# Attention and the output projection of one decoder layer on one core: the product with v a step later, row turnings inside the products

## The chip, the cores and the metric

The kernel runs on one core of one Trainium2 chip. The metric is the device time of one execution in microseconds; the times shown are medians of several runs. Lower is better.

## The reference, cut to what matters

One layer of a decoder for 2048 prompt tokens and 8 x 4 decode tokens, all in float32. Attention is "stick breaking": no softmax, but a product over the keys behind.

```python
z = einsum('bqhd,bkhd->bhqk', q, k) * HEAD_DIM_SB ** -0.5 + sb_bias
mask = k_pos[None, :] < q_pos[:, None]
log_1mb = where(mask, log_sigmoid(-z), 0.0)
suffix = cumsum(log_1mb, axis=3, reverse=True) - log_1mb
a = where(mask, exp(log_sigmoid(z) + suffix), 0.0)
o = einsum('bhqk,bkhd->bqhd', a, v)
...
hp = hp + mix_merge(o_sb, o_mlp, gn_sb, gn_mlp, w_out)      # two RMS norms, one projection
y, conv_p = conv_ffn(rmsnorm(hp), ...); hp = hp + y          # 1024 -> 2 x 2816 -> 1024
hp = per_layer_embedding(hp, p, ...)
y_prompt = rmsnorm(hp, final_norm_g)
```

There are 8 heads of 64; the decode tokens attend to 2048 cached keys, held in pages of 128 that a page table names.

## The kernel before, in words

Four stages follow each other: `project_mlp`, `project_qk`, `attend`, `finish_tokens`. Products in full precision are made of float32 operands split into a high and a low part (`k_hi`, `k_lo`, `w_hi`, `w_lo`): ScalarE casts the high part, VectorE subtracts it for the low part, and TensorE makes two or three products.

**attend.** One step is one block of 128 queries of one head against its i + 1 tiles of 128 keys (i = 0 to 15); there are 128 steps, written out by hand, and every engine walks through them in order. Step t does several things for different blocks. TensorE makes the logits of block t into `ps_z` (`logits`, L959 to L963), turns the weights of block t - 3 in groups of four tiles into the three banks `ps_t` (`turn`, L969), and makes their product with v into `ps_o` (`weigh`, L981). ScalarE makes two sigmoids out of each bank pair of logits (L1104, L1106), copies each turned group from `ps_t` to `aT` (`take`, L1093) and each finished quad of blocks to `oT` (`quad_out`, L1116). VectorE runs the scan over the keys of block t - 1 (`product`, L1211) and the weights of block t - 2 (`weights`, L1216). One turned group goes ahead of the logits (up to three, where no keys are turned), the others behind them; the product with v follows at once.

The decode tokens are worked in the same steps, in two groups of four sequences of 54 units each, spread over the steps by a count of keys (`units_of`, at most a few units a step): 32 units of key pages (TensorE turns two pages a unit, L991, ScalarE copies one and VectorE the other, L1284; every fourth unit also makes logits, L1001), one for the new keys, one scan, one for the weights, two for turning, 16 sums with v pages (L1034; VectorE adds each to `own`, L1268) and one mix. All turned blocks, keys, logits and sums share the three banks in one fixed order (`fill_at`). GpSimd issues the page loads (L930) into a ring of 9 pages, each when the page 9 before it has been used. SP loads the q and k of a whole head (`load`, L870: four pieces of 512 KB) into one raw buffer once the previous head's are split; ScalarE casts k at i = 5 (`keys_high`, L1111), VectorE splits q at i = 5 to 7 and k at i = 8 (L1185 to L1206).

**finish_tokens.** Five blocks of 416 tokens. Per block: the output projection in 8 products of 8 k-tiles x 3 matmuls (L58 to L60, `product`), the feed-forward pair, and the embedding gate. Weights arrive in slabs of 512 KB; ScalarE casts them (`high`, L1568), VectorE subtracts (`low`, L1729), four slots each. The finished rows of block b - 1 leave during the output projection of block b: VectorE normalises 8 tiles (L1796), then, between the fourth and fifth product, `turn_out` turns them in 8 groups of four into two banks (L1487), and ScalarE's `way_out` copies each group (L1630) and issues its store (L1635). VectorE then adds the residual (L1751), which frees the accumulator that the fifth product needs.

Of the kernel before, what the change touches and what calls it, by code (L numbers as in the profile page):

```python
# [700 lines left out]
def attend(nc, keep, T, D):  # L701
# [4 lines left out]
    GROUPS, PB, PAGES, RING = 2, 4, 16, 9  # L706
# [5 lines left out]
    HIGH_PARTS, LOW_PART = 5, 8  # L712
    FIRST = BANK

    def has(s):
        return 0 <= s < STEPS
# [21 lines left out]
    units_of = [[] for _ in range(STEPS + LAG + 1)]  # L738
    t, run, placed = 3, keys_of(3) + 300, 0
    for g in range(GROUPS):  # L740
        for u in range(UNITS):
            if apart(u) and units_of[t]:
                t += 1
                run += keys_of(t) + 300
# [36 lines left out]
    for t in range(STEPS + LAG):  # L781
# [7 lines left out]
    with ExitStack() as ctx:  # L789
        m = Alloc(nc, ctx, "at")  # L790
        k_raw, q_raw = m.sb("k_raw", [P, 2048]), m.sb("q_raw", [P, 2048])
# [4 lines left out]
        aT = [m.sb(f"aT{s}", [P, 4, P]) for s in range(4)]  # L796
# [8 lines left out]
        v_new = m.sb("v_new", [4 * PB, GROUPS, BANK])  # L805
# [12 lines left out]
        loaded, k_high, head_high, head_low, z_ready, b_done, product_done, a_done = (  # L818
            m.sem(n) for n in ("loaded", "k_high", "head_high", "head_low", "z_ready", "b_done", "product_done", "a_done"))
        o_ready, o_out, made, cast, rest_zeroed = (m.sem(n) for n in ("o_ready", "o_out", "made", "cast", "rest_zeroed"))  # L820
        first_loaded, first_k_high, first_q_high, first_ready = (
            m.sem(n) for n in ("first_loaded", "first_k_high", "first_q_high", "first_ready"))
# [7 lines left out]
        v_src = T["v_prompt"][0, 0].rearrange("(kt p) h d -> p kt h d", p=P)  # L830
        caches = [T[n][0].rearrange("n p h d -> p n (h d)") for n in ("cache_k", "cache_v")]
# [31 lines left out]
        with nc.Block() as block:  # L863

            @block.sync
            def _(sp):
                def load(h):
                    for raw, src in ((k_raw, D["KT"]), (q_raw, D["QT"])):
                        for half in range(2):
                            sp.dma_start(raw[64 * half:64 * half + 64, :], src[64 * h:64 * h + 64, :]).then_inc(loaded, 16)  # L870

                def load_first(raw, src, c0, c1, signal):
                    for half in range(2):
                        sp.dma_start(raw[64 * half:64 * half + 64, c0:c1], src[0:64, c0:c1]).then_inc(signal, 16)
# [9 lines left out]

                load_first(k_raw, D["KT"], 0, FIRST, first_loaded)
                load_first(k_raw, D["KT"], FIRST, 2048, loaded)
# [1103 lines left out]
```

## Time and profile before

| | |
|---|---|
| median of 3 runs | 3399.02 us (3394.91 to 3401.98) |
| the profiled execution, its own time | 3402.7 us |
| its span | 3401.1 us |
| mean granted TensorE clock | 0.975 |
| TensorE busy | 3206.0 us |
| VectorE busy | 2106.0 us |
| ScalarE busy | 1645.8 us |

The span runs from the first to the last instruction. Busy time is the union of an engine's instructions; matmuls are pipelined, so that a record lasts longer than the distance to the next one, and a busy TensorE isn't one at its peak. PE is TensorE, DVE VectorE, ACT ScalarE, POOL GpSimd; L981 is line 981 of the kernel.

### The profile page before, as it was taken

What the parts mean: (1) busy time and instruction counts of PE and PEld (TensorE: products, weight loads), DVE (VectorE), ACT (ScalarE), POOL (GpSimd) and SP (SyncE); (2) the same over time, 40 slices, a digit from 0 to 9 for tenths busy, and PEclk for the clock granted to TensorE, in tenths of its full rate; (3) what the DMA queues carried; (4) which work ended last, traced back from release to release, by engine and by line L of the source; (5) the groups of instructions that cost most, each with busy time, mean ns of one, the idle gap of its engine ahead of it and who ended that gap; (6) DMA issues with size and microseconds to landing.
All of it is one profiled execution on the core that took longest, in us unless ns stands there. A gap on an engine that the chain in (4) does not pass through costs nothing.

```text
span 3401.1 us, 51867 instructions
## 1 busy us (share of the span) xinstructions
PE 3206.0 (94%) x18462; PEld 2941.2 (86%) x18462; DVE 2106.0 (62%) x2865; ACT 1645.8 (48%) x2305; POOL 146.5 (4%) x275
## 2 busy tenths in 40 slices
PE   8999897788989989799999999999999999999997
PEld 6888686677777767699998999899998999989996
DVE  4222322678877787577476764777656775678845
ACT  5434211676667666445344443454444543445433
POOL 0000000111221111000000000000000000000000
PEclk9999898899999999899999999999999999999998
DMA  5222334642654333543444333543335433433331
GB/s 174 91 93 71 117 108 116 160 106 71 168 145 111 98 106 97 169 123 115 116 136 141 117 113 113 154 126 118 110 104 171 122 117 113 141 115 116 115 116 59
DMA packets 575191, 405.62 MB, mean 119 GB/s; under 512 B 37498, under 2 KB 538659, under 8 KB 573187
## 3 DMA queue, kind: packets, MB, share of 16 engines
q1 hardware_dynamic: 532660, 298.24, 30.7%
q0 software_dynamic: 20480, 67.13, 6.8%
q10 hardware_dynamic: 21872, 37.92, 3.3%
q8 instruction: 108, 1.77, 0.2%
q14 instruction: 71, 0.57, 0.1%
HBM read 358.34 MB, written 44.87 MB: 119 GB/s over the span
## 4 chain that ended last, share of the span: by engine, by line
PE 57%; DVE 1%; ACT 1%; issue 0%; ACTq 0%; DMA 0%; DVEq 0%
PE pf_acc L60 19%; PE pf_acc L58 19%; PE pf_acc L59 18%; PE pf_ps_sum L1449 0%; ACTq L1635 0%; ACT pf_c L1630 0%; DMA pf_mix<-MIXT 0%; ACT pf_u L1630 0%; PE pf_ps_t L1487 0%; DVE pf_h L1914 0%; DVE pf_u L1735 0%; ACT pf_sq L1575 0%; DVE pf_h L1751 0%; DVE pf_h L1796 0%; DVE pf_ssum L1745 0%
## 5 line engine op out<-in xcount | busy, mean ns | idle before, releaser
L58 PE MATMUL pf_acc<-pf_x_hi,pf_w_hi 128*128 128x416 f32 x2080 | 732.0, 352 | 2.4 <-DVE pf_h L1751 2.4
L60 PE MATMUL pf_acc<-pf_x_hi,pf_w_lo 128*128 128x416 f32 x2080 | 734.2, 353 | 0.0
L1568 ACT ACTIVATE pf_w_hi<-pf_raw 128x1024 fp32r<-128x1024 f32 x440 | 464.7, 1057 | 541.8 <-PE pf_acc L60 538.7
L59 PE MATMUL pf_acc<-pf_x_lo,pf_w_hi 128*128 128x416 f32 x2080 | 725.9, 349 | 0.0
L1729 DVE TENSOR_TENSOR pf_w_lo<-pf_raw,pf_w_hi 128x1024 fp32r<-128x1024 f32 x440 | 536.8, 1221 | 283.0 <-ACT pf_w_hi L1568 282.8
L58 PE MATMUL pf_acc<-pf_f_hi,pf_w_hi 128*128 128x416 f32 x1280 | 456.4, 357 | 11.1 <-DVE pf_w_lo L1729 8.0
L60 PE MATMUL pf_acc<-pf_f_hi,pf_w_lo 128*128 128x416 f32 x1280 | 455.7, 356 | 0.0
L59 PE MATMUL pf_acc<-pf_f_lo,pf_w_hi 128*128 128x416 f32 x1280 | 451.3, 353 | 0.0
L59 PEld LDWEIGHTS pf_acc<-pf_x_lo,pf_w_hi 128*128 128x128 f32 x2080 | 390.8, 188 | 8.1 <-issue 1.6
L58 PEld LDWEIGHTS pf_acc<-pf_x_hi,pf_w_hi 128*128 128x128 f32 x2080 | 390.4, 188 | 7.1 <-issue 5.0
L60 PEld LDWEIGHTS pf_acc<-pf_x_hi,pf_w_lo 128*128 128x128 f32 x2080 | 390.0, 188 | 2.2
L1211 DVE TENSOR_TENSOR_SCAN at_rest<-at_rest 128x127 f32<-128x127 f32 (+15 forms) x128 | 309.2, 2416 | 26.3 <-ACT at_rest L1106 26.0
L981 PE MATMUL at_ps_o<-at_aT,at_v 128*64 128x128 f32 x2176 | 276.7, 279 | 45.9 <-ACT at_aT L1093 41.6
L981 PEld LDWEIGHTS at_ps_o<-at_aT,at_v 128*64 128x64 f32 x2176 | 237.0, 138 | 71.5 <-ACT at_aT L1093 51.7
L58 PEld LDWEIGHTS pf_acc<-pf_f_hi,pf_w_hi 128*128 128x128 f32 x1280 | 243.7, 190 | 17.2 <-DVE pf_w_lo L1729 9.2
L59 PEld LDWEIGHTS pf_acc<-pf_f_lo,pf_w_hi 128*128 128x128 f32 x1280 | 243.8, 190 | 5.5 <-issue 1.3
L60 PEld LDWEIGHTS pf_acc<-pf_f_hi,pf_w_lo 128*128 128x128 f32 x1280 | 243.3, 190 | 1.8
L1093 ACT ACTIVATE at_aT<-at_ps_t 128x512 f32<-128x512 f32 (+2 forms) x320 | 157.8, 536 | 136.8 <-PE at_ps_t L969 136.5
L969 PE MATMUL at_ps_t<-keep_ident,at_rest 128*128 128x128 f32 x1088 | 159.5, 282 | 28.9 <-DVE at_rest L1216 28.3
L1104 ACT ACTIVATE at_beta<-at_ps_z,at_bias 128x1024 f32<-128x1024 f32 (+2 forms) x192 | 166.6, 868 | 25.9 <-PE at_ps_z L960 16.4
L969 PEld LDWEIGHTS at_ps_t<-keep_ident,at_rest 128*128 128x128 f32 x1088 | 122.2, 144 | 63.8 <-DVE at_rest L1216 47.5
L58 PE MATMUL pa_ps_acc<-pa_w_hi,pa_x_hi 128*128 128x512 f32 x408 | 164.6, 403 | 6.8 <-DVE pa_w_lo L480 6.8
(225 smaller groups left out, 4394.3 us busy)
## 6 DMA issues: line engine op xcount, KB each, us to landing
pf_raw<-in_w_up_dram SPq DMA_DIRECT2D x220, 512.0 KB, 3.8
pf_raw<-in_w_down_dram SPq DMA_DIRECT2D x80, 512.0 KB, 4.0
at_pages<-in_cache_k_dram POOLq DMA_DIRECT2D x128, 256.0 KB, 3.2
at_pages<-in_cache_v_dram POOLq DMA_DIRECT2D x128, 256.0 KB, 3.2
pf_raw<-in_w_out_dram SPq DMA_DIRECT2D x40, 512.0 KB, 5.2
pf_raw<-in_w_ple_gate_dram SPq DMA_DIRECT2D x40, 512.0 KB, 4.0
pf_raw<-in_w_down_dram SPq DMA_DIRECT2D x40, 384.0 KB, 3.4
pf_mix<-MIXT ACTq DMA_DIRECT2D x5, 1664.0 KB, 9.4
```

Source lines behind the costliest of these rows:

```text
L58: nc.tensor.matmul(out, stat_hi, mov_hi, start=first, stop=False)
L59: nc.tensor.matmul(out, stat_hi, mov_lo, start=False, stop=False)
L60: return nc.tensor.matmul(out, stat_lo, mov_hi, start=False, stop=last)
L969: last = nc.tensor.transpose(bank[:, kt % 4 * P:kt % 4 * P + P], rest[s % 4][:, kt * P:(kt + 1) * P], keep["ident"][:, :])
L981: last = nc.tensor.matmul(ps_o[0:64, i % 4 * P:(i % 4 + 1) * P], v[h % 2][:, kt, :], aT[group(s, r) % 4][:, kt % 4, :], start=kt == 0, sto ...
L1093: nc.scalar.activation(out, src, ACT.Copy).then_inc(emptied_by(key), 1)
L1104: nc.scalar.activation(beta[t % 3][:, 1024 * g:1024 * g + w], ps_z[at % 2][:, 0:w], ACT.Sigmoid, bias=bias[t // NQ % 2][:, :])
L1211: nc.vector.tensor_tensor_scan(r, r, r, 1.0, ALU.mult, ALU.min).then_inc(product_done, 1)
L1568: nc.scalar.activation(w_hi[k % 4][:, :], raw[k % 4][:, :], ACT.Copy).then_inc(hi_split, 1)
L1729: nc.vector.tensor_tensor(w_lo[k % 4][:, :], raw[k % 4][:, :], f32(w_hi[k % 4][:, :]), ALU.subtract).then_inc(lo_split, 1)
```

## The change

In `attend`, the product with v of block s is made one step later (`weigh(s - 1)`), and all turned groups of a step stand in one run ahead of the logits. `aT` gets 8 slots instead of 4. ScalarE makes all copies out of the three banks: both pages of a key unit, and each sum, which goes to a buffer `stage` that VectorE then adds from, behind its scan and weights. q and k are loaded, cast and split by halves of 1024 columns into raw buffers of half the size: the first half of the next head at i = 10 to 12, the second half of the current head at i = 4 to 6. The ring has 8 pages instead of 9, and `v_new` is loaded by GpSimd, per group. In `finish_tokens`, the 8 groups of turnings stand inside the third, fourth and fifth product (`TURNS`), the first half of the tiles first, each followed by its own copy and store on ScalarE; VectorE adds the residuals of the first four tiles as soon as that half is turned and makes their low parts one tile behind.

```diff
-    GROUPS, PB, PAGES, RING = 2, 4, 16, 9
+    GROUPS, PB, PAGES, RING = 2, 4, 16, 8
...
-    HIGH_PARTS, LOW_PART = 5, 8
-    FIRST = BANK
+    HALF, FIRST = 1024, BANK
+    PART_AT = (10, 4)
+    SLOTS = 8
...
-        return min(groups[s], max(1, 3 - len(turned_fills(t)))) if has(s) else 0
+        return groups[s] if has(s) else 0
...
-        k_raw, q_raw = m.sb("k_raw", [P, 2048]), m.sb("q_raw", [P, 2048])
+        k_raw, q_raw = m.sb("k_raw", [P, HALF]), m.sb("q_raw", [P, HALF])
...
-        aT = [m.sb(f"aT{s}", [P, 4, P]) for s in range(4)]
+        aT = [m.sb(f"aT{s}", [P, 4, P]) for s in range(SLOTS)]
...
-                def load(h):
+                def load(n):
+                    h, c0 = n // 2, n % 2 * HALF
+                    sp.wait_ge(half_ready, n)
...
+                    if h + 1 < HEADS:
+                        load(2 * h + 2)
                     store(h, 0)
                     store(h, 1)
-                    if h + 2 < HEADS:
-                        sp.wait_ge(head_low, h + 2)
-                        sp.wait_ge(head_high, 3 * h + 6)
-                        load(h + 2)
+                    if h + 1 < HEADS:
+                        load(2 * h + 3)
...
+                                if part == 1 and k + bi == 0:
+                                    if g:
+                                        wait_filled(pool, ("sum", g - 1, PAGES - 1))
+                                    pool.dma_start(v_new[:, :], new_rows[16 * g:16 * g + 16, :]).then_inc(new_loaded, 16)
...
+                    if i == (4 if h == 0 else 0) and g == 0:
+                        pe.wait_ge(half_ready, 2 * h + 1)
+                    if i == 8 and g == 0:
+                        pe.wait_ge(half_ready, 2 * h + 2)
...
-                        weigh(s)
+                    if has(s - 1):
+                        weigh(s - 1)
...
+                def keys_high(n):
+                    h, c0 = n // 2, n % 2 * HALF
+                    act.wait_ge(loaded, 64 * n + 64)
+                    nc.scalar.activation(k_hi[h % 2][:, c0:c0 + HALF], k_raw[:, :], ACT.Copy).then_inc(k_high, 1)
...
+                    if U_SUM <= u < U_MIX:
+                        key, n = ("sum", g, u - U_SUM), PAGES * g + u - U_SUM
+                        if n >= 2:
+                            act.wait_ge(summed, n - 1)
+                        wait_filled(act, key)
+                        nc.scalar.activation(stage[n % 2][:, :], bank_of(key)[:, :], ACT.Copy).then_inc(emptied_by(key), 1)
...
+                        for bi in (2 * (u % 2), 2 * (u % 2) + 1):
+                            k, key = u // 2, ("key", g, u // 2, bi)
+                            copy_out(key, kT[:, bi, :, k % 2 * P:k % 2 * P + P], bank_of(key)[:, :].rearrange("p (h t) -> p h t", h=4))
...
-                    if quad_end(s - 1):
-                        quad_out((s - 1) // 4)
+                    if quad_end(s - 2):
+                        quad_out((s - 2) // 4)
...
+                    if t % NQ == PART_AT[0] and t // NQ + 1 < HEADS:
+                        keys_high(2 * (t // NQ + 1))
+                    if t % NQ == PART_AT[1] and t < STEPS:
+                        keys_high(2 * (t // NQ) + 1)
...
+                def operands(n, part, first=0):
+                    slot = n // 2 % 2
+                    src = slice(first, HALF)
+                    cols = slice(n % 2 * HALF + first, n % 2 * HALF + HALF)
                     if part == 0:
-                        dve.wait_ge(loaded, 64 * h + 64)
-                        done = nc.vector.tensor_copy(q2[slot][:, c0:], q_raw[:, c0:])
-                    elif part == 1:
-                        dve.wait_ge(head_high, 3 * h + (1 if h else 2))
-                        done = nc.vector.tensor_tensor(q2[slot][64:P, c0:], q_raw[64:P, c0:], f32(q2[slot][64:P, c0:]), ALU.subtract)
-                    else:
-                        nc.vector.tensor_scalar(bias[slot][:, :], keep["sb_bias"][:, h:h + 1], 1.0, None, ALU.mult)
-                        done = nc.vector.tensor_scalar(minus_bias[slot][:, :], keep["sb_bias"][:, h:h + 1], -1.0, None, ALU.mult)
-                    done.then_inc(head_high, 1)
+                        dve.wait_ge(loaded, 64 * n + 64)
+                        nc.vector.tensor_copy(q2[slot][:, cols], q_raw[:, src]).then_inc(q_high, 1)
+                    if part == 1:
+                        dve.wait_ge(q_high, n + 1)
+                        nc.vector.tensor_tensor(q2[slot][64:P, cols], q_raw[64:P, src], f32(q2[slot][64:P, cols]), ALU.subtract)
+                        if n % 2 == 0 and n:
+                            biases_of(n // 2)
+                    if part == 2:
+                        dve.wait_ge(k_high, n + 1)
+                        nc.vector.tensor_tensor(k_lo[slot][:, cols], k_raw[:, src], f32(k_hi[slot][:, cols]), ALU.subtract).then_inc(half_ready, 1)
...
-                        k, bi = u // 2, 2 * (u % 2) + 1
-                        key = ("key", g, k, bi)
-                        wait_filled(dve, key)
-                        nc.vector.tensor_copy(kT[:, bi, :, k % 2 * P:k % 2 * P + P], bank_of(key)[:, :].rearrange("p (h t) -> p h t", h=4))\
-                            .then_inc(emptied_by(key), 1)
...
+                    for g, u in units_of[t - 1] if t else ():
+                        sample_sums(g, u)
+                    if t == 1:
+                        for part in range(3):
+                            operands(0, part, FIRST)
+                    for half in range(2):
+                        part, h = t % NQ - PART_AT[half], t // NQ + 1 - half
+                        if 0 <= part < 3 and h < HEADS:
+                            operands(2 * h + half, part)
...
+    TURNS = {2: {5: 0, 7: 1}, 3: {1: 2, 3: 3, 5: 4, 7: 5}, 4: {1: 6, 3: 7}}
...
+                        if i == 7:
+                            last.then_inc(slab_done, 1)
+                        if i in groups:
+                            turn_out(b, groups[i])
...
-                        if mt == 4 and behind:
-                            turn_out(b - 1)
...
+                def turn_out(b, n):
+
+                    half, tt = divmod(n, 4)
+                    w = P if tt < 3 else 32
+                    pe.wait_ge(y_ready, 8 * b + 4 * half + 4)
+                    pe.wait_ge(y_copied, 8 * b + n + 1)
+                    for k in range(4):
+                        done = nc.tensor.transpose(ps_t[n % 2][0:w, k * P:(k + 1) * P], h[:, 4 * half + k, tt * P:tt * P + w], keep["ident"][:, :])
+                    done.then_inc(y_turned, 1)
...
+                        for cast, groups in ((4, ()), (5, (0, 1)), (6, (2, 3))):
+                            high(q4, O_AT + cast)
+                            for n in groups:
+                                way_out(b - 1, behind_at, False, n)
                     for mt in range(8):
                         residual(b, 0, mt, OU, G_FFN, (q4, O_AT + mt + 4) if mt >= 4 or behind_at is None else None)
+                        if behind_at is not None and mt < 4:
+                            if mt == 1:
+                                high(q4, O_AT + 7)
+                            way_out(b - 1, behind_at, False, 4 + mt)
...
+                    if norm == 0 and mt % 4 == 0 and not isinstance(b, int):
+                        dve.wait_ge(y_turned, 8 * b + mt - 3)
...
+                    for mt in range(4 if behind else 0):
                         done(q4, O_AT + mt)
-                        residual(b, 0, mt, OU, G_FFN, (q4, O_AT + mt + 4) if mt >= 4 or not behind else None)
+                        add_residual(b, 0, mt, OU)
+                        if mt:
+                            low_residual(b, 0, mt - 1, G_FFN)
+                    if behind:
+                        low_residual(b, 0, 3, G_FFN)
+                        low(q4, O_AT + 7)
```

## Rows read from the trace of the kernel before

**Rows 1.** Busy us, share of the span and instructions, from the page.

```profile
PE 3206.0 (94%) x18462; PEld 2941.2 (86%) x18462; DVE 2106.0 (62%) x2865; ACT 1645.8 (48%) x2305; POOL 146.5 (4%) x275
```

**Rows 2.** Windows of two stages: length, busy us per engine, clock, DMA share, GB/s.

```profile
588.00:1368.00 780.00, 689.37 (x5442) 558.96 (x5442) 582.45 (x414) 524.85 (x836) 138.02 (x256) 0.96 0.44 118
1368.00:3401.00 2033.00, 1971.02 (x10324) 1926.93 (x10324) 1343.53 (x2093) 930.31 (x1152) 0.13 (x1) 0.98 0.42 123
```

**Rows 3.** TensorE's waits from 588 to 1368: us in total, times, longest.

```profile
PE at_ps_o L981 <- ACT at_aT L1093: 41.6, 36, 10.6
PE at_ps_t L969 <- DVE at_rest L1216: 28.3, 16, 6.6
...
PE at_ps_t L1034 <- DMA at_pages<-in_cache_v_dram: 6.4, 4, 5.0
PE at_ps_t L991 <- DMA at_pages<-in_cache_k_dram: 5.1, 1, 5.1
```

**Rows 4.** Timeline of TensorE, one step: start, us, instructions [idle before].

```profile
727.46 0.43 PE L981 MATMUL at_ps_o<-at_aT,at_v 128*64 128x128 f32 x2 [1.13 <-ACT at_aT L1093]
727.82 1.09 PE L991 MATMUL at_ps_t<-keep_ident,at_pages 128*128 128x128 f32 x8
...
730.75 1.09 PE L981 MATMUL at_ps_o<-at_aT,at_v 128*64 128x128 f32 x8
732.77 0.65 PE L981 MATMUL at_ps_o<-at_aT,at_v 128*64 128x128 f32 x4 [0.93 <-ACT at_aT L1093]
733.35 1.09 PE L991 MATMUL at_ps_t<-keep_ident,at_pages 128*128 128x128 f32 x8
```

**Rows 5.** Timeline of ScalarE in the same step.

```profile
729.39 0.60 ACT L1093 ACTIVATE at_aT<-at_ps_t 128x512 f32<-128x512 f32 x1 [0.28 <-PE at_ps_t L969]
...
731.34 1.11 ACT L1106 ACTIVATE at_rest<-at_ps_z,at_minus_bias 128x1023 f32<-128x1023 f32 x1
732.33 0.38 ACT L1093 ACTIVATE at_aT<-at_ps_t 128x256 f32<-128x256 f32 x1
```

**Rows 6.** Last stage, turning of rows: three windows (as rows 2), then two copies of ScalarE.

```profile
1797.24:1807.77 10.53, 6.34 (x35) 3.78 (x34) 1.82 (x2) 5.11 (x8) 0.00 (x0) 0.77 0.76 241
1807.77:1813.13 5.36, 5.36 (x15) 5.11 (x16) 2.26 (x5) 2.75 (x5) 0.00 (x0) 0.50 0.25 89
1813.13:1818.49 5.36, 5.36 (x30) 5.29 (x29) 3.94 (x9) 3.16 (x6) 0.00 (x0) 0.99 0.00 0
...
1798.15 0.60 ACT L1630 ACTIVATE pf_c<-pf_ps_t 128x512 f32<-128x512 f32 x1 [3.99 <-PE pf_ps_t L1487]
...
1799.39 0.60 ACT L1630 ACTIVATE pf_c<-pf_ps_t 128x512 f32<-128x512 f32 x1 [0.64 <-ACT pf_c L1630]
```

**Rows 7.** Timeline of TensorE at the end of the kernel.

```profile
3384.14 6.79 PE L1487 MATMUL pf_ps_t<-keep_ident,pf_h 128*128 128x128 f32 x28 [1.13 <-DVE pf_h L1796]
```

**Rows 8.** Head 0: TensorE's timeline, then a window (as rows 2).

```profile
620.28 1.97 PE L981 MATMUL at_ps_o<-at_aT,at_v 128*64 128x128 f32 x8 [10.63 <-ACT at_aT L1093]
...
620.30:626.00 5.70, 5.70 (x25) 4.95 (x25) 5.33 (x5) 3.28 (x5) 0.87 (x2) 0.56 0.05 15
```

**Rows 9.** VectorE in attention, by line: busy us, mean ns, idle before.

```profile
L1211 DVE TENSOR_TENSOR_SCAN at_rest<-at_rest 128x127 f32<-128x127 f32 (+15 forms) x128 | 309.2, 2416 | 26.3 <-ACT at_rest L1106 26.0
...
L1284 DVE COPY at_kT<-at_ps_t 128x512 f32<-128x512 f32 x64 | 44.2, 691 | 108.2 <-PE at_ps_t L991 108.1
```

**Rows 10.** Head 1: its window (as rows 2), and TensorE's waits in it.

```profile
695.50:792.50 97.00, 90.14 (x744) 74.73 (x744) 71.84 (x52) 68.88 (x110) 15.02 (x28) 0.98 0.41 109
...
PE at_ps_o L981 <- ACT at_aT L1093: 6.1, 7, 1.4
PE at_ps_t L969 <- DVE at_rest L1216: 2.1, 1, 2.1
```

**Rows 11.** Landings: all loads of L870 (512 KB each), and one kind of DMA.

```profile
DMA to landing us min/median/max: 5.2/9.6/15.1
...
at_k_raw<-KT SPq DMA_DIRECT2D x2, 128.0 KB, 3.8
```

More of the change, by code:

```diff
@@ L737, in attend @@
     total_keys = sum(keys_of(s) + 300 for s in range(3, STEPS - 2))
-    units_of = [[] for _ in range(STEPS + LAG + 1)]
+    units_of = [[] for _ in range(STEPS + LAG + 2)]
     t, run, placed = 3, keys_of(3) + 300, 0
@@ L742, in attend @@
             if apart(u) and units_of[t]:
-                t += 1
-                run += keys_of(t) + 300
+                for _ in range(2 if u == U_MIX else 1):
+                    t += 1
+                    run += keys_of(t) + 300
             while t < STEPS - 3 and run * GROUPS * UNITS < placed * total_keys:
@@ L804, in attend @@
         q_block, k_new = m.sb("q_block", [P, 4, PB, 32]), m.sb("k_new", [P, 4, 4 * PB])
-        v_new = m.sb("v_new", [4 * PB, GROUPS, BANK])
+        v_new = m.sb("v_new", [4 * PB, BANK])
+        stage = [m.sb(f"stage{n}", [P, BANK]) for n in range(2)]
         beta_s, rest_s = m.sb("beta_s", [P, KEYS + 4]), m.sb("rest_s", [P, KEYS + 4])
@@ L1069, in _ @@
                 pe.wait_ge(cast, 2)
-                for t in range(STEPS + LAG):
+                for t in range(STEPS + LAG + 1):
                     s = t - LAG
@@ L1146, in _ @@
                 act.sem_inc(oT_stored[1], 16)
-                for c0, c1, signal in ((0, FIRST, first_loaded), (FIRST, 2048, loaded)):
-                    for half in range(2):
-                        act.dma_start(q_raw[64 * half:64 * half + 64, c0:c1], D["QT"][0:64, c0:c1]).then_inc(signal, 16)
+                for c0, c1, signal in ((0, FIRST, first_loaded), (FIRST, HALF, loaded)):
+                    for part in range(2):
+                        act.dma_start(q_raw[64 * part:64 * part + 64, c0:c1], D["QT"][0:64, c0:c1]).then_inc(signal, 16)
                 nc.scalar.activation(warm[:, :], keep["eps"][:, :], ACT.Sigmoid)
@@ L1153, in _ @@
                 act.wait_ge(rest_zeroed, 4)
-                for t in range(STEPS + LAG + 1):
+                for t in range(STEPS + LAG + 2):
                     s = t - LAG
@@ L1299, in _ @@
                 first_operands()
-                for t in range(STEPS + LAG + 1):
-                    for g, u in units_of[t - 1] if t else ():
-                        sample_sums(g, u)
+                for t in range(STEPS + LAG + 2):
                     for g, u in units_of[t]:
@@ L1455, in mix_mean_square, with product @@
                     nc.tensor.matmul(ps_sum[:, 0:TB], keep["mean512"][:, :], c[0][:, 0:TB], start=True, stop=True).then_inc(mix_sum, 1)
-                def product(q4, k, unit, mov_hi, mov_lo, order=range(8), ready=None):
+                def product(q4, k, unit, mov_hi, mov_lo, order=range(8), ready=None, groups={}, b=None):
                     for i, kt in enumerate(order):
@@ L1549, in _ @@
                 mean_square(21 * NB)
-                turn_out(NB - 1)
+                for n in range(8):
+                    turn_out(NB - 1, n)
                 for n in range(6):
@@ L1713, in _ @@
                 root(NB - 1, 2)
-                way_out(NB - 1, (NB - 1) * TB, True)
+                for n in range(8):
+                    way_out(NB - 1, (NB - 1) * TB, True, n)
                 for n in range(6):
@@ L1758, in residual @@
                     add_square(b, norm, mt)
+                def residual(b, norm, mt, unit, gain, between=None):
+                    add_residual(b, norm, mt, unit)
+                    if between and mt < 7:
+                        low(*between)
+                    low_residual(b, norm, mt, gain)
                     if between and mt == 7:
```

151 lines of the change are left out of this document (50 added, 101 removed).

## The prediction

> **What bounds the kernel now.** I read the page's busy table first. TensorE is busy 94% of the span [rows 1], so what counts is where TensorE stands still. The windows by stage put that in one place: between 588 and 1368 us (attention) TensorE is busy 689.4 of 780 us, VectorE 582.5, ScalarE 524.9; in the last stage it is busy 1971 of 2033 us [rows 2]. The diff touches those two stages and no other.
>
> The waits of TensorE inside attention [rows 3] say what ends its pauses. 41.6 us in 36 pauses end with ScalarE's copy of a turned block: the product with v of a step follows its own turnings at once. 28.3 us in 16 end with VectorE's weights; 6.4 and 5.1 us end with pages that land late.
>
> The timeline of one middle step [rows 4] shows the mechanism. TensorE turns keys at 727.82, starts the product with v at 730.75, runs out after eight matmuls and goes on only at 732.77; the next step starts at 733.35. The eight show 1.09 us busy and two show 0.43; the six more cost 0.66, 0.11 each. The ninth could have begun at 730.75 + 8 x 0.11 = 731.63; the real loss is 1.14 against 0.93 shown. I add 0.2 to each such pause. ScalarE [rows 5] is then inside two sigmoids of 1024 (1.11 each, 1.0 apart) and reaches the last block's copy at 732.33.
>
> In the last stage I looked for the same thing at the turning of the finished rows, once per block of tokens [rows 6]. From 1797.24 to 1807.77 there is no product at all: eight groups of four turnings alternate with ScalarE's copies, whose starts are 1.24 apart. Then 15 matmuls take 5.36 us at a granted clock of 0.50 (1.2 GHz); the next 30 take the same time at 0.99 (2.4 GHz).
>
> **The last stage, costed.** After the change the eight groups stand inside the third, fourth and fifth product, two k-tiles apart. Removed per block: 10.53 us, and the slow start after it, 15 matmuls of 0.36 instead of 0.18, 2.7 us. Added: 32 turnings between products. Four turnings are issued in about 0.5 us (eight key turnings of the same size show 1.09 in rows 4 like eight products with v, so 0.12 each), so 8 x 0.5 = 4.0. The gate of the groups is ScalarE: copy 0.6 and DMA issue 0.4 make 1.24 per group; groups are 6 x 0.18 + 0.5 = 1.6 apart on TensorE, so ScalarE keeps up while it has nothing else. It also has two casts and the residual's two passes over a tile, each about as long as a copy or two, between the groups from the third on. Following its order, only the eighth group's bank is late, by some 0.4; I take 0.7. Sum per block: 10.53 + 2.7 - 4.0 - 0.7 = 8.5, four times 34. VectorE's new order (residual 0 only after group 4 of the first half) frees the fifth product's bank about 2 us before it is wanted. At the end of the kernel the groups go half by half, so that the first four need only four normalised tiles: the second group waited 1.13 more for the other half [rows 7], 1.2 gained. **35 us**, bounds 26 (each group at ScalarE's pace once more: 2 us a block) and 38.
>
> For the slow start: the Trainium skill (TensorE: Matmul & The Clock Gate, Terms) gives the penalty of a throttled time as that time times (1 - K/N), here one half. Applied to the throttled time of a block, which reaches back into the turnings (0.77 in the 10.53 us before, rows 6), it would give more than the 2.7 us that the row shows. By the row, only the throttled part in which products run dense counts, and I go by the row.
>
> **Attention, what is removed.** (a) 35 of the 36 pauses behind ScalarE's copies, 31.0 us, plus 0.2 each, 7: 38. Product s-1 uses copies made a step ago, and eight slots of aT keep them.
> (b) The 36th, 10.63 us at 620.28, is something else: ScalarE had to cast head 1's k and, in order behind that, copy this step's block; the load of 2 MB landed late [rows 8]. Now 1 MB is wanted at that point, it is released sooner (operands of the first half are ready at step 1, not 3, and SP no longer issues v_new in front of it), and 1 MB of head 0 is no longer ahead of it. I leave 2.5 us of it: 8 gained, bounds 4 and 10.6. After it TensorE ran 5.7 us at a clock of 0.56, 2.5 us lost, gained too. The page wait of 5.1 just before: 2 gained.
> (c) VectorE's 28.3 us. Its scans, 309 us, and the weights stay [rows 9]. It no longer copies half the keys (44 us) and no longer stands behind TensorE's key turnings (108 us idle, rows 9), so it starts on a step's scan earlier. The longest, 6.6 us, stands behind the scan of the decode part; there are two such, 13 us, and they stay. Of the other 15 us I take half, 8; bounds 3 and 15.
> (d) Pages of v, 6.4 us, in 4 pauses, the longest 5.0, while a 2 MB head load was under way: 3 gained; a ring of 8 pages instead of 9 gives at most 2 us back at the step with two sums.
> Removed: 38 + 8 + 2.5 + 2 + 8 + 3 = 61.5.
>
> **Attention, what is added.** ScalarE gets 64 key copies and 32 copies of sums. In a run they start 0.5 apart (0.60 shown; an instruction of 1.11 in rows 5 is followed after 0.99, so some 0.1 overlaps), 48 us over the stage; 525 + 48 = 573 of about 735. In head 1 [rows 10] TensorE needs 97.0 less its stops of 6.1 + 2.1 and 8 x 0.2: 87.2; ScalarE 68.9 + 14 x 0.5 = 76; VectorE 71.8 - 14 x 0.6 = 63.5. TensorE stays the bound over the head, but not in each step. With 9 to 13 key tiles ScalarE has 1.0 (keys) + 1.0 to 1.3 (blocks) + 2.0 + 0.5 to 1.4 (sigmoids), and 0.95 more where half of k is cast (1024 columns, like a sigmoid of rows 5): 4.2, 4.6, 5.8, 5.3, 5.6. TensorE has 4.1 (733.35 - 727.82 = 5.53 in rows 4, less the stop of 1.14 and one tile less to weigh), 4.5, 4.9, 5.4, 5.9. All turnings come before the logits and share three banks, so a late ScalarE stops TensorE at its fourth fill. Following both through these steps, stops of 0.25, 0.7, 1.15 and 0.25 come out, and the hand-over of a bank (0.28 idle in rows 5) adds about 0.1 a step: 3.5 per full head of key pages, of which there are five: **17.5** given back. This is an estimate; bounds 5 (banks always free) and 45 (a stop of 1 us in most of the 45 steps with key pages from 8 tiles up). VectorE's adds of sums stay as long as they are and lie in its idle time. Halved casts cost the same elements plus some 0.2 each, hidden on ScalarE and VectorE. One extra step at the end costs nothing: the same product, its copies already made.
> Net attention: 61.5 - 17.5 = **44**.
>
> **Sum.** 35 + 44 = 79. The profiled execution took 3402.7 us (span 3401.1), the runs' median is 3399.0, 0.1% less. 3402.7 - 79 = 3323.7; against the median **3320**.
>
> **Rivals.** *ScalarE becomes the bound of attention.* Its added 48 us lie in front of the turn that TensorE wants next. For it: step 10 above, 5.8 against 4.9. Against: 76 against 87.2 per head. It gives back 45 instead of 17.5: net 79 - 27.5 = 51, 3348.
> *Better than thought.* VectorE's pauses go altogether (7 more) and banks are always free (12.5 more): 79 + 19.5, 3300. For it: VectorE's idle of 108 us behind key turnings.
> *The half loads land late.* A half is now issued at about step 6 and cast at step 10, 15.3 us later by the steps above; issuing its four pieces takes about 2, and landings of the 512 KB pieces were 5.2 to 15.1 us [rows 11]. At 15.1 each, 2 us are lost in seven heads, 14 in all: 3334. Against: half the bytes. The Trainium skill (DMA: Bandwidth & Descriptors, Measured) asks for batches of at least 1 MiB and so speaks against cutting 512 KB into 256 KB; by the rows a 128 KB piece still took 3.8 us where the median of 512 KB was 9.6, so fixed cost is there, but the slack covers it.
> *Slower than before: the run of turnings goes in lockstep.* Place: the 320 blocks and 128 key pages through three banks ahead of the logits. If each fill waited for the copy of the one before, a fill would cost 0.60 + 0.28 instead of 0.49: 0.39 x 448 = 175 us, 3495. It decides once half of the fills pay it (87 us eats the 79). For it: the interleaving with the logits, which hid this, is gone. Against: three banks, and ScalarE's 0.5 pitch in a run equals TensorE's fill.
>
> **How the numbers follow.** Forecast 0.62, ScalarE the bound 0.15, better 0.12, late halves 0.05, lockstep 0.06 (a third of it ends within the bound below). The predicted time is the first case's. Its own range is 3306 to 3336. From 3296 to 3352 four cases fit, and with their tails and the bounds of (b), (c) and the bank stops this should hold 8 in 10. 0.2%, 7 us, is about what a measurement of this kernel can tell from no change: faster by more 0.94, within 0.02, slower 0.04.
>
> **What would show it.** In the profile after: no product with v waits for an aT copy; turnings wait for ScalarE's copies instead, some 15 to 20 us in pauses under 1.2; the 10.6 us pause near 620 is 3 or less; attention lasts about 736 us. Each of four blocks is 8.5 us shorter, without a stretch at 0.50 clock after it. ScalarE busy rises by about 55 us in attention, VectorE's falls by some 45. The prediction is wrong if waits on the banks pass 45 us, if VectorE's pauses at the start of a head grow, or if groups inside products wait for ScalarE by more than a microsecond each.

## The result, and the profile after

The changed kernel takes **3347.1 us** (median of 4 runs, 3346.6 to 3349.3) against 3397.0 (4 runs, 3393.4 to 3402.0): a ratio of 0.9853, 95% interval 0.9836 to 0.9871. The forecast was 3320, in a range of 3296 to 3352. So 50 us came where 79 were forecast. By the two profiled executions it is 56 (3401.1 - 3344.9 us): that of the kernel before lay 5.7 us above its median, that of the changed kernel 0.3 below. The stages below are read from those two, so they have some 6 us more to share out than the medians.

The page of the changed kernel, its busy line:

```profile
PE 3187.5 (95%) x18462; PEld 2933.7 (88%) x18462; DVE 2067.2 (62%) x2823; ACT 1682.2 (50%) x2411; POOL 148.3 (4%) x277
```

Two windows of it, attention and the last stage (columns as rows 2; the last stage begins with its first instruction on TensorE, at 1371.50 before and at 1350.82 now):

```profile
588.00:1343.70 755.70, 690.15 (x5441) 562.77 (x5439) 544.62 (x371) 562.09 (x941) 139.09 (x257) 0.97 0.44 121
...
1350.82:3344.90 1994.08, 1951.63 (x10324) 1915.37 (x10324) 1342.37 (x2093) 928.80 (x1152) 0.00 (x0) 0.99 0.43 125
```

The last stage took 3401.1 - 1371.5 = 2029.6 us and takes 1994.1: 35.5 less, forecast 35. Attention ends 1371.50 - 1350.82 = 20.7 us sooner, forecast 44: the traces are 23 us short of the forecast. By the medians attention gave only some 14 (50 less the 36 of experiment 1). TensorE's waits inside attention, after (to set against rows 3):

```profile
PE at_ps_t L976 <- DVE at_rest L1237: 21.9, 12, 6.9
PE at_ps_t L1041 <- DMA at_pages<-in_cache_v_dram: 20.9, 9, 5.8
PE at_ps_o L988 <- ACT at_oT L1125: 7.9, 8, 1.3
PE at_ps_t L976 <- ACT at_kT L1101: 6.5, 14, 1.0
PE at_ps_o L988 <- issue: 3.5, 7, 0.5
PE at_ps_t L976 <- ACT at_rest_s L1101: 1.8, 3, 0.8
PE at_ps_t L998 <- DMA at_pages<-in_cache_k_dram: 1.8, 2, 1.2
```

The line that led before, the product behind the copies of aT (41.6 us), is gone. The line for v pages (L1041, 6.4 before) is now 20.9. The first two lines together (42.8 us) cost more than all stops behind ScalarE's copies (16.7).

Where a step is held up by ScalarE, its timeline and TensorE's look like this (head 1, around the cast of half of the next k; the stop falls in the step after it). TensorE first:

```profile
719.86 1.74 PE L988 MATMUL at_ps_o<-at_aT,at_v 128*64 128x128 f32 x14
721.53 1.09 PE L998 MATMUL at_ps_t<-keep_ident,at_pages 128*128 128x128 f32 x8
722.46 0.60 PE L976 MATMUL at_ps_t<-keep_ident,at_rest 128*128 128x128 f32 x4
724.10 0.81 PE L976 MATMUL at_ps_t<-keep_ident,at_rest 128*128 128x128 f32 x5 [1.03 <-ACT at_kT L1101]
```

```profile
722.02 0.59 ACT L1114 ACTIVATE at_rest<-at_ps_z,at_minus_bias 128x384 f32<-128x384 f32 x1
722.48 1.07 ACT L1120 ACTIVATE at_k_hi<-at_k_raw 128x1024 fp32r<-128x1024 f32 x1
723.43 1.10 ACT L1101 ACTIVATE at_kT<-at_ps_t 128x512 f32<-128x512 f32 x2
724.38 1.28 ACT L1101 ACTIVATE at_aT<-at_ps_t 128x512 f32<-128x512 f32 x3
```

The product of 14 matmuls runs through (1.74 us). TensorE then fills its three banks in a row, keys twice and one group of turnings, and stands at the fourth fill for 1.03 us until the first key copy (723.43) has freed a bank; that copy waited behind the sigmoids and the cast. The prediction put 1.15 us there.

The last stage, groups of turnings among products, and at the end of the kernel:

```profile
1770.64 0.35 PE L60 MATMUL pf_acc<-pf_f_hi,pf_w_lo 128*128 128x416 f32 x1
1770.83 0.60 PE L1494 MATMUL pf_ps_t<-keep_ident,pf_h 128*128 128x128 f32 x4
1771.18 0.44 PE L58 MATMUL pf_acc<-pf_f_hi,pf_w_hi 128*128 128x416 f32 x1
...
1782.53 0.60 PE L1494 MATMUL pf_ps_t<-keep_ident,pf_h 128*32 128x128 f32 x4 [0.56 <-ACT pf_c L1635]
...
3327.08 4.79 PE L1494 MATMUL pf_ps_t<-keep_ident,pf_h 128*128 128x128 f32 x20 [5.86 <-DVE pf_h L1812]
```

A group holds the next product matmul back from 1770.83 to 1771.18, 0.35 us, and the one after that follows at 0.28 instead of 0.19; in all a group costs 0.44 (groups are 1.57 apart, with six matmuls of 0.19 between them). Seven groups of a block pass without a wait and the eighth waits 0.56; it is the same in each of the four blocks.

The v pages, at the longest stop (head 3): TensorE's timeline, SP's before it, and three windows (columns as rows 2).

```profile
936.32 1.94 PE L1041 MATMUL at_ps_t<-at_pages,at_rest_s 128*32 128x512 f32 x8 [5.85 <-DMA at_pages<-in_cache_v_dram]
```

```profile
925.02 1.14 SPq L876 DMA_DIRECT2D at_k_raw<-KT  x2
926.20 1.63 SPq L876 DMA_DIRECT2D at_q_raw<-QT  x2
```

```profile
930.47:936.32 5.85, 0.00 (x2) 0.03 (x1) 5.85 (x4) 0.60 (x1) 2.14 (x4) 0.91 1.02 279
936.32:941.32 5.00, 5.00 (x22) 1.68 (x23) 1.10 (x3) 0.72 (x2) 0.00 (x0) 0.50 0.31 117
941.32:950.00 8.68, 8.68 (x53) 7.64 (x52) 2.38 (x3) 6.48 (x9) 2.15 (x4) 0.76 0.42 122
```

A megabyte of q and k is issued at 925.02 to 927.8 among the pages. While TensorE waits, all DMA engines are busy (share 1.02, 279 GB/s). The four pieces are two of k and two of q, 256 KB each; the view of the DMA issues gives the median time to landing over attention, the view of the page loads' line (L936) their least, median and most:

```profile
at_pages<-in_cache_v_dram POOLq DMA_DIRECT2D x128, 256.0 KB, 3.3
at_pages<-in_cache_k_dram POOLq DMA_DIRECT2D x127, 256.0 KB, 3.3
at_k_raw<-KT SPq DMA_DIRECT2D x30, 256.0 KB, 4.6
at_q_raw<-QT SPq DMA_DIRECT2D x30, 256.0 KB, 6.6
```

```profile
DMA to landing us min/median/max: 2.8/3.3/10.1
```

Before, the same loads (L930) had this, so pages as a whole don't land later; what counts is which of them do.

```profile
DMA to landing us min/median/max: 2.7/3.2/13.6
```

After the stop the granted clock is 0.50 for 5.0 us and 0.76 for the next 8.7, so the stop costs more than its 5.85 us.

### The profile page after: what moved, and what is told of

It reads as the page before. It is cut to its first block, busy times and chain, and to the rows that moved or that the text cites. A ratio compares the mean times of both kernels' runs of the same rounds, so it can differ in the third digit from the quotient of the medians.

```text
span 3344.9 us, 52003 instructions
## 1 busy us (share of the span) xinstructions
PE 3187.5 (95%) x18462; PEld 2933.7 (88%) x18462; DVE 2067.2 (62%) x2823; ACT 1682.2 (50%) x2411; POOL 148.3 (4%) x277
## 3 DMA queue, kind: packets, MB, share of 16 engines
q1 hardware_dynamic: 535172, 298.70, 31.3%
## 4 chain that ended last, share of the span: by engine, by line
PE 56%; ACT 1%; DVE 1%; issue 1%; DMA 0%; ACTq 0%; DVEq 0%
PE pf_acc L60 19%; PE pf_acc L58 19%; PE pf_acc L59 18%; PE pf_ps_sum L1457 0%; DMA pf_mix<-MIXT 0%; ACT pf_c L1635 0%; ACT pf_sq L1582 0%; ACTq L1640 0%; PE pf_ps_t L1494 0%; ACT pf_w_hi L1575 0%; DVE pf_h L1937 0%; DVE pf_u L1744 0%; DVE pf_h L1760 0%; DVE pf_ssum L1754 0%; ACT pf_u L1635 0%
## 5 line engine op out<-in xcount | busy, mean ns | idle before, releaser
L988 PE MATMUL at_ps_o<-at_aT,at_v 128*64 128x128 f32 x2176 | 266.2, 276 | 11.6 <-ACT at_oT L1125 7.9
L976 PE MATMUL at_ps_t<-keep_ident,at_rest 128*128 128x128 f32 x1088 | 156.5, 286 | 31.2 <-DVE at_rest L1237 21.9
```

What stands on the lines that cost most here:

```text
L976: last = nc.tensor.transpose(bank[:, kt % 4 * P:kt % 4 * P + P], rest[s % 4][:, kt * P:(kt + 1) * P], keep["ident"][:, :])
L988: last = nc.tensor.matmul(ps_o[0:64, i % 4 * P:(i % 4 + 1) * P], v[h % 2][:, kt, :], aT[group(s, r) % SLOTS][:, kt % 4, :], start=kt == 0, ...
```

## The experiments

The kernel before took 3400.4 us beside experiments 1 to 4, 3398.6 beside 5, 6, 8 and 9, and 3397.8 beside 7 and 10 to 12. Waits and busy times are TensorE's, within attention. As the kernel before moved by 3 us from one set of runs to the next, a difference to after of 4 us or less is not certain by the times alone. Busy time moves too: the attention of before had 689.4 us in its own trace and 685.6 in that of experiment 1.

**1. The last stage alone**: attention of before with the last stage of after.

> Attention as before, the last stage as after. If the last stage gave what the prediction costed (35.5 us by the two profiles), this comes out at 3397 - 35 = 3362, and the change's attention is worth only the rest, 15 us. Rival: part of the 35 us comes only because attention ends differently; then it gives less than 30.

Measured: 3364.4 us, ratio 0.9898 (0.9881 to 0.9914), 36 us. The last stage is worth what was forecast; what is missing, is missing in attention, which by this gives some 14 us.

**2. A ring of nine pages again.**

```diff
-    GROUPS, PB, PAGES, RING = 2, 4, 16, 8
+    GROUPS, PB, PAGES, RING = 2, 4, 16, 9
```

> The changed kernel with a ring of 9 pages instead of 8. Theory A (the ring makes the v pages late): the waits for v pages fall from 20.9 us to the 6.4 of before and the time falls by about 12 to 15 us, to 3333. Theory B (the DMA engines are full while a half head load runs beside the pages): one page more ahead changes the waits by 4 us at most, time 3343 to 3347.

Measured: 3343.4, ratio 0.9838 (0.9822 to 0.9855). Waits for v pages are 19.0 us in 5 pauses instead of 20.9 in 9. One page less in the ring explains about 4 us of time and 1.9 of these waits, so the ring isn't what made most of them.

**3. The half-head loads later**: the first half of the next head is issued one store later and its operands are made two steps later.

```diff
-                    if h + 1 < HEADS:
-                        load(2 * h + 2)
                     store(h, 0)
+                    if h + 1 < HEADS:
+                        load(2 * h + 2)
                     store(h, 1)
...
-    PART_AT = (10, 4)
+    PART_AT = (12, 4)
```

> The changed kernel, but the first half of the next head is loaded after the store of quad 0 (about step 8, not 6) and cast and split at steps 12 to 14, not 10 to 12, so that it doesn't run beside the pages of the short steps. Theory B: the waits for v pages near 887 and 900 us go, 5 to 8 us less in all, time 3339 to 3342; the operands also leave the steps with 9 to 11 tiles, in which ScalarE was late. Theory A: no change in the waits for pages.

Measured: 3336.5, ratio 0.9815 (0.9798 to 0.9831), 11 us less than after, more than expected. Waits for v pages fall to 15.9, behind key copies to 3.9, and TensorE's busy time from 690.2 to 685.4. Added up over windows of 2 us, the low clock holds for about 38 us of attention instead of 53. The stops did not go where they were expected to: that near 887 stays (2.21), the 2.77 near 900 becomes 5.98, and it is the 5.85 of head 3 and the 5.51 of head 6 that fall to 1.19 and 1.31. The later operands also move the issue of the second halves (925.02 becomes 941.68).

**4. The half-head loads nearly empty.** After the first two, each loads 64 of its 1024 columns, and q and k of the later heads are made mostly from old values. The instructions stay the same.

```diff
-sp.dma_start(raw[64 * part:64 * part + 64, :], src[64 * h:64 * h + 64, c0:c0 + HALF]).then_inc(loaded, 16)
+c1 = HALF if n < 2 else 64
+sp.dma_start(raw[64 * part:64 * part + 64, 0:c1], src[64 * h:64 * h + 64, c0:c0 + c1]).then_inc(loaded, 16)
```

> The changed kernel, but of each half head load of q and k after the first two only 64 of 1024 columns are loaded, so head 1 and later compute with old columns: it leaves out nearly all of the DMA traffic of these loads and nothing else. Theory B: the waits for v pages fall from 20.9 to under 6 us and the time by 15 us. Theory A: they stay above 15 us.

Measured: 3329.3, ratio 0.9791 (0.9775 to 0.9807), 18 us less. Waits for v pages are 11.2 us (expected under 6), none over 2.5, and TensorE's busy time is 683.8, 6.3 less, with about 36 us at the low clock instead of 53. In this kernel the loads of the next head cost 18 us by the DMA engines they share with the pages: about 10 in stops, 6 in matmuls that run slower after them. The 11.2 us that stay are not the loads' bytes.

**5. The product in its own step again**, the run of turnings kept.

```diff
-                    if has(s - 1):
-                        weigh(s - 1)
+                    if has(s):
+                        weigh(s)
...
-                    if quad_end(s - 2):
-                        quad_out((s - 2) // 4)
+                    if quad_end(s - 1):
+                        quad_out((s - 1) // 4)
```

> The changed kernel, but the product with v is made in the same step as its turnings again (and the quad copied a step earlier); the turnings stay in one run ahead of the logits. Theory C (the delay by a step is what removed the 31 us of waits for ScalarE's copies, with 7 us of hidden loss): those waits come back, time 25 to 38 us more, 3372 to 3385. Rival D (it was the run: all copies now stand ahead of the sigmoids on ScalarE, so they are done by the time the logits are): at most 8 us more, 3347 to 3355.

Measured: 3333.2, ratio 0.9808 (0.9792 to 0.9825): 14 us *faster* than after, which neither theory had. The product waits for copies of aT only 8.3 us in 5 pauses, of which 5.2 is the one of head 0.

**6. The turnings split again**, the delay kept: one to three groups ahead of the logits, the rest behind.

```diff
-        return groups[s] if has(s) else 0
+        return min(groups[s], max(1, 3 - len(turned_fills(t)))) if has(s) else 0
```

> The changed kernel, but as before only one to three turned groups go ahead of the logits and the rest behind them; the product with v stays a step later. Theory C: the delay does it alone, so the time stays within 4 us of 3347; ScalarE's late copies fall behind the sigmoids, but nobody waits for them in the step. Theory D: waits for copies come back, 10 us or more.

Measured: 3334.7, ratio 0.9811 (0.9795 to 0.9827), 12 us faster than after, again outside both theories: no product waits for a copy of aT.

**7. Both undone**: edits 5 and 6 together. Halves, copies on ScalarE, staged sums and the last stage stay.

> After, with weigh back in its own step and first_turns back to one to three groups, so with neither the delay nor the run of turnings; halves, the key copies on ScalarE, the staged sums and the last stage stay as in after. It is the fourth cell of a table: both 3347, the run alone 3333, the delay alone 3335 us. Theory D (either one alone removes the product's waits for aT, some 38 us in before, and each costs some 13 us of its own once the other has done it): the waits of the product for the copies of aT come back at about 30 us in some 35 places, ScalarE's key-copy stops (3 us) go, and the time is 3355 to 3370 us. Rival (the product's waits of before came mostly from VectorE's key copies or the whole-head loads, which are gone here as well, so neither the delay nor the run was needed): 3325 to 3340 us, with under 12 us of aT waits.

Measured: 3355.9, ratio 0.9869 (0.9852 to 0.9885). The waits came back, as its waits and its window (columns as rows 2) show:

```profile
PE at_ps_o L988 <- ACT at_aT L1101: 31.3, 34, 5.7
PE at_ps_t L976 <- DVE at_rest L1237: 17.2, 6, 6.5
PE at_ps_t L1041 <- DMA at_pages<-in_cache_v_dram: 17.0, 9, 4.7
```

```profile
588.00:1355.00 767.00, 692.86 (x5442) 559.92 (x5442) 544.92 (x372) 566.09 (x941) 141.01 (x258) 0.96 0.44 120
```

And the waits with the run alone (5), then with the delay alone (6):

```profile
PE at_ps_t L1041 <- DMA at_pages<-in_cache_v_dram: 17.2, 7, 4.8
PE at_ps_t L976 <- DVE at_rest L1237: 16.7, 6, 6.5
...
PE at_ps_o L988 <- ACT at_aT L1101: 8.3, 5, 5.2
...
PE at_ps_o L988 <- ACT at_oT L1125: 7.2, 16, 0.8
PE at_ps_t L976 <- ACT at_kT L1101: 3.3, 4, 0.8
```

```profile
PE at_ps_t L976 <- DVE at_rest L1237: 23.6, 14, 6.9
PE at_ps_t L1041 <- DMA at_pages<-in_cache_v_dram: 22.5, 10, 6.4
...
PE at_ps_o L988 <- issue: 3.5, 7, 0.5
PE at_ps_t L998 <- DMA at_pages<-in_cache_k_dram: 3.5, 3, 1.7
PE at_ps_o L988 <- ACT at_oT L1125: 2.4, 3, 1.0
...
PE at_ps_t L976 <- ACT at_aT L1101: 0.8, 2, 0.4
```

The four cells side by side, in us (aT: the product behind copies of aT; banks: turnings behind any of ScalarE's copies; o bank: product behind the copy of its bank, with the 0.5 us "issue" pauses at the same instruction):

| | median | busy | aT | VectorE | v pages | banks | o bank |
|---|---|---|---|---|---|---|---|
| neither | 3355.9 | 692.9 | 31.3 | 17.2 | 17.0 | 0.8 | 6.1 |
| run alone | 3333.2 | 685.4 | 8.3 | 16.7 | 17.2 | 4.3 | 7.2 |
| delay alone | 3334.7 | 683.9 | 0 | 23.6 | 22.5 | 2.5 | 5.9 |
| both (after) | 3347.1 | 690.2 | 0 | 21.9 | 20.9 | 8.8 | 11.4 |

Each of the two cures alone takes 21 to 23 us off. The second one on top gives 12 to 14 of them back. There was one pause to cure, and either cures it: with the run, all copies come ahead of the sigmoids, so they are ready when the product comes; with the delay, they are a step old.

One stop changes its column from cell to cell. In head 0 the second half of its own q and k lands late (with both cures VectorE stands 5.36 us for it and ScalarE 4.45), and TensorE stands for it in every cell. First after, then the run alone:

```profile
604.96 1.11 PE L976 MATMUL at_ps_t<-keep_ident,at_rest 128*128 128x128 f32 x4 [3.73 <-DVE at_rest L1237]
```

```profile
602.96 1.54 PE L988 MATMUL at_ps_o<-at_aT,at_v 128*64 128x128 f32 x6 [5.21 <-ACT at_aT L1101]
```

It is 5.7 of the 31.3 and 5.2 of the 8.3 us under aT, and 4.5 of the 21.9 under VectorE (3.73 and, just before, 0.76). Without it the product waits 25.6 us with neither cure and 3.1 with the run, and VectorE's waits in after are 17.4, about the 16.7 of the run alone.

**8. VectorE copies every second key page again**, in after.

> The changed kernel, but VectorE copies the second page of each key unit again, ahead of its scan, and so waits for TensorE's key turnings in order. Theory E (VectorE standing behind those turnings is what made it late at the start of a head): the stops of 2.1 us at the start of heads return and TensorE's waits for the weights grow from 21.9 to about 30 us, while its 6.5 us of waits for ScalarE's key copies go; 0 to 6 us more, 3347 to 3353. Rival (ScalarE's load costs more than VectorE's order): 5 us less or better, under 3342.

Measured: 3351.0, ratio 0.986 (0.9843 to 0.9876), 4 us slower than after by the medians, 2 by the ratios; in the traces attention is 4.6 us longer. VectorE's waits rise from 21.9 to 29.3 us and those behind ScalarE's key copies fall only from 6.5 to 5.3. This part of the change most likely earns its place, though the times alone don't settle it.

**9. Late loads and nine pages** (2 and 3 together).

> The changed kernel with both: the first half of the next head loaded and split later, and a ring of 9 pages. If the two act on the same waits for pages through different causes (bytes beside the pages, pages ahead), their gains of 11 and 4 us add up to 12 to 15, time 3332 to 3335; if they act on one cause, no better than 3336.

Measured: 3327.1, ratio 0.9788 (0.9771 to 0.9804), 20 us less than after; waits for v pages 8.7. The two give more together than 11 + 4, and more than either expectation. It would fit that a page more in the ring helps once the loads are out of its way; no run shows that by itself.

**10. 9 with the product in its own step**, and **11. 9 with the turnings split.**

> The best parts together: the half-head loads two steps later, a ring of nine pages, and weigh in its own step. If the three savings lie in different places (20 us at v-page sums, 14 at the deferred product), the time is 3333 - 20 = 3313 us (3308 to 3320), with some 9 us of v-page waits. If they share their time (a head bound by its page transfers gains nothing from a shorter TensorE path), it is 3320 to 3327, and the v-page waits grow to 15 us or more.

> The same loads and ring with the delayed product, but the turnings of a step split as in before (one to three groups ahead of the logits). By the sum 3335 - 20 = 3315 us (3310 to 3322); the longest waits of the split version were for v pages (22.5 us, the most of all versions), so if it shares its time with them the gain of the loads is larger here: 3308 to 3312.

Measured: 3313.9, ratio 0.975 (0.9733 to 0.9766), and 3313.0, ratio 0.9745 (0.9729 to 0.9761). The savings add up (3333 - 20 and 3335 - 20), as they do when they lie in different places.

**12. 10 with four tiles for aT and twelve pages.** Without the delay no copy has to last into the next step.

```diff
-    GROUPS, PB, PAGES, RING = 2, 4, 16, 9
+    GROUPS, PB, PAGES, RING = 2, 4, 16, 12
...
-    SLOTS = 8
+    SLOTS = 4
```

> late9_same with four tiles for aT in place of eight and twelve pages in the ring (the same memory in all but one page). If the remaining v-page waits (about 9 us) are bursts that a deeper ring covers, they fall under 3 us and the time is 5 to 7 us under that of late9_same, near 3307. If they are the full rate of the transfers over several steps, or if eight tiles for aT covered a wait (then waits of the turning copies for the product appear), it is within 3 us of late9_same or above it.

Measured: **3305.9**, ratio 0.9734 (0.9717 to 0.9751), the fastest, 41 us under after (three runs lie within 0.5 us, the fourth is 3313.3). Its waits and its window:

```profile
PE at_ps_t L976 <- DVE at_rest L1237: 17.3, 8, 6.5
...
PE at_ps_t L1041 <- DMA at_pages<-in_cache_v_dram: 0.8, 1, 0.8
```

```profile
588.00:1309.00 721.00, 678.96 (x5437) 557.93 (x5436) 544.53 (x371) 563.88 (x941) 140.16 (x257) 0.98 0.45 127
```

The v-page waits are all but gone, and TensorE's busy time is 11 us under after's. They were bursts, which a deeper ring covers, and the memory for it was in the second set of aT tiles, which only the delay needs.

## Why the prediction was right, and where it was off

The direction, the range and the last stage were right; attention was forecast 23 us too good by the traces, 30 by the medians. None of its signs of being wrong came: the waits on the banks stayed far under 45 us, VectorE's pauses at the starts of heads shrank (2.12 us in head 1 before, none over 0.15 after) and no group waited for over a microsecond. 3347 is almost the 3348 of the rival in which ScalarE bounds attention, and lies outside the likeliest case's own range of 3306 to 3336, but it did not get there by that rival's way. That it stayed inside the stated range is in part luck: 9 us too much charged for the banks made up for some of what was missed elsewhere. The bill of its terms, by TensorE's waits before and after:

| term | forecast | measured |
|---|---|---|
| (a) 35 pauses behind copies of aT | -31 | -31.0 |
| (a) 0.2 more in each, (b) 2.5 of slow clock | -9.5 | +0.8 |
| (b) pause of head 0 | -8 | -6.1 |
| (b) pages of k | -2 | -3.3 |
| (c) VectorE | -8 | -10.9 |
| (d) pages of v | -3 | +14.5 |
| stops at the banks | +17.5 | +8.3 |
| the bank of the product | 0 | +8.3 |
| sum | -44 | -19.4 |

(The measured column is busy time for the second line, waits for the others; a wait for head 0's v of 0.5 us went too; the start of the last stage says -20.7.)

**(d) is the term that failed most**, 17.5 of the 23 us; the busy time of the second line missed by 10.3 and the bank of the product by 8.3, against 9.2 too much for the banks. The prediction took the 5.0 us pause of before for the work of the 2 MB head load and let it go with it. It is still there, at the same step of head 3, as 5.85 (rows above), and there are more: 5.51 in head 6, and 2.18, 2.77 and 1.47 in head 3 and before it. The same bytes are still moved while v pages come at the rate that the sums want, and now half of them are issued earlier: in head 3 at 888.08 and 925.02, where before all 2 MB stood at 935.46. Experiments 3, 4 and 9 showed that the greater part is these loads: all but emptying them takes 9.7 us of the 20.9 away and 18 us of time. Experiment 2 showed that the smaller ring had 1.9 of the waits. With the loads emptied 11.2 us stay, where before had 6.4 with full loads; what makes this rest was not found. The delay and the run are not needed for it: the cell with neither has 17.0. The rival of late half loads looked at the wrong end of this: it asked whether the halves land in time for their casts. They do; the only such wait is in head 0, for its own second half. What came late were the pages beside them. For the size of a transfer, the Trainium skill (DMA: Bandwidth & Descriptors, Measured) asks for batches of at least 1 MiB. Here the cut did not hurt by itself: the 256 KB pieces of k and q land after 4.6 and 6.6 us in the median, the 512 KB pieces took 7.7 and 12.1 (all together 9.6 [rows 11]): half the bytes in 0.6 and 0.55 of the time.

**(a) was right in size, wrong in what it needs.** All 31 us went. But the prediction gave the credit to the delay; the four cells show that the run of turnings alone does it too. It costed the two parts as one cure plus its price, and never asked what the one is worth once the other is there. Its 0.2 us per pause would fit the 7.5 us less busy time for the run alone and 9.0 for the delay alone, but both together have only 2.7 less (690.2 against 692.9), and one and the same attention differed by 3.8 between two traces, so it is not shown.

**(b), (c)** held within 3 us. The pause of head 0 is now 3.73 and 0.76 us behind VectorE, whose scan stands behind the operands of head 0's second half, and these behind its load. The clock after it is still low, though (0.50 from 605 to 611), so those 2.5 us stayed. The two stops at the scan of the decode part are 6.92 each.

**The stops at the banks** are 6.5 us behind key copies, 1.8 and 0.5 behind the others: half of the 17.5, far from the 45 of the rival in which ScalarE bounds attention, and farther from lockstep. In head 1 they are 0.33, 0.22, 0.22 and 1.03, where 0.25, 0.7, 1.15 and 0.25 were followed through, plus 0.1 a step for the hand-over of a bank, which shows as no wait. ScalarE's own bill was too high as well: its busy time in attention rose by 37 us (524.9 to 562.1), where 55 were expected.

**The bank of the product** was not in the sum. At the start of each head ScalarE copies out the finished o bank only after all groups of the run, and TensorE, a step later with its product, stands 0.95 us before it, seven times, and 1.27 once at the end; 0.5 us of "issue" comes on top in the fifth step. With the turnings split the first goes (7.9 to 2.4 us); without the delay the second does.

**The last stage** was right, term by term within half a microsecond a block. From the last mean square (L1449, L1457) before the groups to the next, the four blocks took 51.0, 51.5, 49.9 and 49.8 us and take 42.0, 42.8, 42.3 and 41.3: 8.5 less on average, as forecast. A group costs 0.44 us among products, not 0.5, and the eighth waits 0.56 (forecast 0.7); against that stand small stops of the products that were not forecast, 0.4 in the first block, 1.2 in the second and 0.8 in the third. At the end of the kernel the eight groups and their copies take 0.7 us less than before: the wait for the second half is gone, but later groups wait for ScalarE (0.32, 0.44, 0.44). What follows them is another 0.7 shorter, so the end gives 1.4, forecast 1.2.

What stays open: why both cures together cost 12 to 14 us. Of the 16 us by which attention with both is longer than with the run alone, 10.8 are waits (VectorE 5.2, v pages 3.7, banks 4.5, o bank 4.2, less 8.3 for aT, and 1.5 for k pages, not in the table) and 4.7 busy time. The stop of head 0 stands in these under several names (with the k pages next to it 6.3 us with both, 5.5 with the run alone); without it VectorE has 0.7, and aT -3.1. So v pages, banks and the o bank carry the waits, and only the o bank is traced to its cause. The low clock has a part in the busy time against the run alone (TensorE is busy in it for about 39 us with both, 33 with the run alone), but none against the delay alone (39 in each, 6.2 us less busy time), which stays unexplained.

## What to carry to other kernels

When two parts of a change cure the same wait, run each alone: here either takes 22 us off and both together 9, and the one that needs twice the buffers was not the one to keep. A transfer that is cut in two and moved earlier is not only to be checked against its own reader: list what else is on the DMA engines at the new place, and who waits for that. And what a wait frees is worth counting in memory too: the tiles that the delay had taken, given to the ring of pages, bought the last 8 us.

## What the runs showed of the hardware

- A stop of 5.85 us on TensorE was followed by 5.0 us at a granted clock of 0.50 and 8.7 at 0.76. In the versions that differ from after in loads and ring alone (after, experiments 2, 3, 9 and 4) the low clock holds for about 53, 49, 38, 38 and 36 us of attention, and TensorE's busy time for the same matmuls is 690.2, 686.6, 685.4, 684.3 and 683.8. Where the order of the matmuls changes, busy time doesn't follow the stops: 683.9 with the delay alone, with 22.5 us of waits for v pages.
- With head loads and pages together the DMA engines were full (share 1.02) at 279 GB/s, where the mean over attention is 121; in head 0, from 600 to 605 us, it was 305 GB/s at a share of 1.09. Pages landed after 3.3 us in the median and 10.1 at the most. Pieces of 256 KB landed in 0.6 (k) and 0.55 (q) of the time of pieces of 512 KB.
- Four turnings set between products cost the products 0.44 us, though they show 0.60 busy.
